# A transformer layer on one core: 31 warm-up products of 32 columns in place of nine of 128, a load in two halves, and a row block of x1 by column halves

## What is computed

```python
h = rmsnorm(x, norm1_g)
z = h @ w_in                       # queries, keys, values, mLSTM inputs and gates
mixed = concat(attention(z), mlstm(z))
x = x + mixed @ w_out              # called x1 below
h2 = rmsnorm(x, norm2_g)
logits = h2 @ w_router + b_router
top_v, top_e = top_k(logits, 4)
gates = softmax(top_v)
for e in range(32):                # the tokens that chose e
    gu = h2[tokens] @ w_gate_up[e] + b_gate_up[e]
    gate, up = min(gu[:, :1024], 7), clip(gu[:, 1024:], -7, 7)
    act = gate * sigmoid(1.702 * gate) * (up + 1)
    y[tokens] += gates[tokens, e] * (act @ w_down[e] + b_down[e])
x = x + y
```

## Time and profile before

| | us |
|---|---|
| median of 3 runs | 1055.46 (1054.89 to 1055.58) |
| the profiled execution, its own time | 1055.73 |
| its span in the profile | 1053.9 |
| TensorE busy | 1037.1 |
| VectorE busy | 197.8 |
| ScalarE busy | 143.0 |
| DMA, mean over the span | 403 GB/s |

### The profile page before, as it was taken

How to read it: one execution, slowest core, us unless ns; L and a number is a source line. 1 busy time by engine, 2 the same in 40 slices (tenths; PEclk the granted TensorE clock), 3 DMA queues, 4 the chain that set the end, 5 groups by cost and what they waited for, 6 DMA issues and landing times.

```text
span 1053.9 us, 11929 instructions
## 1 busy us (share of the span) xinstructions
PE 1037.1 (98%) x4775; PEld 386.1 (37%) x4775; DVE 197.8 (19%) x500; ACT 143.0 (14%) x299; POOL 5.5 (1%) x23
## 2 busy tenths in 40 slices
PE   9999999999999999999999999999999999999997
PEld 5655543333333333333333333333333332333332
DVE  2162332111111111111111111111111111011111
ACT  2144431001111100100111111111110110001101
POOL 1000000000000000000000000000000000000000
PEclk9999999999999999999999999999999999999999
DMA  9964699999999999999999999999999999999997
GB/s 339 364 232 160 254 374 396 428 428 428 428 429 428 429 430 428 428 428 428 428 429 428 430 428 428 428 428 430 428 429 428 428 428 428 429 429 429 425 423 294
DMA packets 42026, 424.62 MB, mean 403 GB/s; under 512 B 6512, under 2 KB 7576, under 8 KB 16536
## 3 DMA queue, kind: packets, MB, share of 16 engines
q1 hardware_dynamic: 41848, 424.10, 96.1%
q10 hardware_dynamic: 160, 0.27, 0.1%
HBM read 423.31 MB, written 1.05 MB: 403 GB/s over the span
## 4 chain that ended last, share of the span: by engine, by line
PE 76%; SPq 16%; DMA 7%; issue 1%; ACT 0%; DVE 0%; POOL 0%; ACTq 0%; POOLq 0%
PE bank L1565 31%; PE bank L1601 16%; SPq L391 9%; PE bank L1175 7%; SPq L398 6%; DMA ring<-in_w_gate_up 5%; PE bank L1524 4%; PE bank L1484 4%; PE bank L1369 3%; PE bank L1422 2%; DMA ring<-in_w_down 2%; PE bank L1495 2%; PE bank L1585 1%; PE bank L1211 1%; PE bank L1576 1%
## 5 line engine op out<-in xcount | busy, mean ns | idle before, releaser
L1565 PE MATMUL bank<-ring,xe_t 128*64 128x512 f32 x2048 | 449.4, 594 | 8.2 <-DMA ring<-in_w_gate_up 7.6
L1565 PEld LDWEIGHTS bank<-ring,xe_t 128*64 128x64 f32 x2048 | 143.0, 137 | 311.0 <-issue 289.6
L1601 PE MATMUL bank<-ring,late 128*64 128x512 f32 x992 | 219.9, 595 | 0.1
L1601 PEld LDWEIGHTS bank<-ring,late 128*64 128x64 f32 x992 | 68.5, 137 | 127.3 <-issue 122.2
L1095 DVE TENSOR_SCALAR gate_c<-bank 128x512 f32<-128x512 f32 x32 | 22.1, 691 | 436.7 <-PE bank L1565 436.7
L775 ACT ACTIVATE s_sb<-bank 128x256 f32<-128x256 f32 x32 | 12.3, 383 | 459.5 <-PE bank L1576 459.5
L1175 PE MATMUL bank<-ring 128*128 128x512 f32 x160 | 72.0, 595 | 0.2 <-issue 0.2
L1524 PE MATMUL bank<-late,s_sb 64*128 64x512 f32 x256 | 63.6, 615 | 0.7 <-ACT late L791 0.7
L1484 PE MATMUL bank<-xres,pick 128*64 128x512 f32 x248 | 60.1, 605 | 0.0
L791 ACT ACTIVATE late<-bank 128x512 f32<-128x512 f32 x32 | 19.1, 597 | 228.2 <-PE bank L1601 228.2
L1093 DVE COPY row_of<-fold 128x64 f32 x31 | 6.0, 195 | 197.1 <-PE bank L1422 197.1
(11 more groups left out here) (210 smaller groups left out, 424.2 us busy)
## 6 DMA issues: line engine op xcount, KB each, us to landing
ring<-in_w_gate_up SPq DMA_DIRECT2D x124, 2048.0 KB, 35.9
ring<-in_w_down SPq DMA_DIRECT2D x59, 2048.0 KB, 32.9
ring<-in_w_in SPq DMA_DIRECT2D x5, 2048.0 KB, 14.7
ring<-in_w_gate_up SPq DMA_DIRECT2D x8, 1024.0 KB, 25.1
ring<-in_w_down SPq DMA_DIRECT2D x7, 1024.0 KB, 24.2
ring<-in_w_out SPq DMA_DIRECT2D x2, 2048.0 KB, 10.6
ring<-in_w_down SPq DMA_DIRECT2D x6, 512.0 KB, 24.0
ring<-in_attn_bias SPq DMA_DIRECT2D x1, 1536.0 KB, 17.8
```

Of the source, the lines that this page charges most:

```text
L1565: mm = pe.matmul(bank[h][c * CAP:(c + 1) * CAP, :], xe_t[:, k, :], w[:, k % RUN, at:at + BANK], start=False, stop=(k == KD - 1), skip_grou ...
L1601: mm = pe.matmul(dst[c * CAP:(c + 1) * CAP, :], turned[:, at:at + CAP], w[:, k % DRUN, c * BANK:(c + 1) * BANK], start=(k == 0), stop=(k = ...
```

## The change

Four edits. Nine warm-up products with 128 moving columns become 31 with 32, the stationary side being the same 128x128 `ones`. The first load of expert 2 (1 MB) is issued as two of 512 KB, each when its columns have been read. The last quarter of x1 (row block 1, column half 1) is added, turned and copied in two halves of 256 columns, the first copy by ScalarE and the second by VectorE, into banks 7 and 0. And around it some places move: `part_copy(1)` stands ahead of `rms_x(1)`, `sum_x(1)` stands inside the top-four code of row block 0, and of the two `dense` products (384 and 256 columns) one with 128 is left.

```diff
-WARM = (5, 4)
+WARM = (16, 15)
...
-                    sp.wait_ge(gu_row_used, 2 * round_no + h + 1)
-                    sp.dma_start(gu_half(s)[:, 0:1, :], rows[:, 0:1, :]).then_inc(ld_piece[s], 16)
+                    if h == 0:
+                        for q in range(2):
+                            sp.wait_ge(gu_row_used, 3 * round_no + q + 1)
+                            sp.dma_start(gu_half(s)[:, 0:1, q * FF:(q + 1) * FF],
+                                         rows[:, 0:1, q * FF:(q + 1) * FF]).then_inc(ld_piece[s], 16)
+                    else:
+                        sp.wait_ge(gu_row_used, 3 * round_no + 3)
+                        sp.dma_start(gu_half(s)[:, 0:1, :], rows[:, 0:1, :]).then_inc(ld_piece[s], 16)
...
             square_x(1, 0)
             part_copy(0)
+            act.wait_ge(h2_turned, 4)
+            act.activation(ht[:, 4:6, P:SEQ], bank[7][:, 0:SEQ].rearrange("p (k n) -> p k n", k=2), ACT.Copy).then_inc(turned_act, 1)
             square_x(1, 1)
-            act.wait_ge(h2_turned, 4)
-            act.activation(ht[:, 4:8, P:SEQ], bank[7][:, :].rearrange("p (k n) -> p k n", k=4), ACT.Copy).then_inc(turned_act, 1)
+            part_copy(1)
             rms_x(1)
-            part_copy(1)
...
+            def add_last_x():
+                dve.wait_ge(mixed, 2 * T)
+                for i in range(2):
+                    xs = xres[:, T - 1, BANK + i * SEQ:BANK + (i + 1) * SEQ]
+                    dve.tensor_tensor(xs, bank[ACC[2 * T - 1]][:, i * SEQ:(i + 1) * SEQ], xs, ALU.add).then_inc(x1_ready, 1)
...
-            add_x(1, 1)
-            sum_x(1)
+            add_last_x()
+            dve.wait_ge(h2_turned, 5)
+            dve.tensor_copy(ht[:, 6:8, P:SEQ], bank[0][:, 0:SEQ].rearrange("p (k n) -> p k n", k=2)).then_inc(turned_dve, 1)
...
                 dve.max(top_v[:, t, :], lg[:, t, :]).then_inc(top_max, 1)
+                if t == 0:
+                    sum_x(1)
...
-                    pe.matmul(bank[1][:, 0:P], ones[:, :], ident[:, :], start=True, stop=True)
+                    pe.matmul(bank[1][:, 0:NE], ones[:, :], ident[:, 0:NE], start=True, stop=True)
...
-            turn_x(1, 1)
+            for i in range(2):
+                pe.wait_ge(x1_ready, 2 * T + i)
+                for k in range(2):
+                    c = 4 + 2 * i + k
+                    mm = pe.transpose(bank[(7, 0)[i]][:, k * P:(k + 1) * P], xres[:, T - 1, c * P:(c + 1) * P], ident[:, :])
+                mm.then_inc(h2_turned, 1)
             fold_parts(0)
-            dense(3 * P)
             logit_part(1, 1)
-            dense(SEQ)
+            dense(P)
             fold_parts(1)
...
+                        if n == 0 and k == 0 and h == 0:
+                            mm.then_inc(gu_row_used, 1)
```

More of the change, by code:

```diff
@@ L100, in loads_before @@
     return TURN_OF[n, k] // PIECES
-IN_HALVES = (piece_of(2, 0), piece_of(2, 1), piece_of(2, GUN))
-PIECE_LOADS = [len(range(s, KINDS * NE, PIECES)) + (s in IN_HALVES) for s in range(PIECES)]
+MORE_LOADS = {piece_of(2, 0): 2, piece_of(2, 1): 1, piece_of(2, GUN): 1}
+PIECE_LOADS = [len(range(s, KINDS * NE, PIECES)) + MORE_LOADS.get(s, 0) for s in range(PIECES)]
 END_PARTS = {(NE - 2, 0): (0, 2), (NE - 2, 1): (0, 2, 3), (NE - 1, 0): (0, 1, 3), (NE - 1, 1): (0, 2, 3)}
@@ L719, in square_x @@
             def square_x(t, c):
-                act.wait_ge(x1_ready, 2 * t + c + 1)
+                act.wait_ge(x1_ready, 2 * t + c + 1 + t * c)
                 if t + c:
@@ L1404, in logit_part @@
                     k = 4 * half + g
+                    if t and k == 6:
+                        pe.wait_ge(turned_dve, 2)
                     mm = pe.matmul(bank[ACC[t]][g * NE:(g + 1) * NE, 0:P], wr[:, k, :], ht[:, k, t * P:(t + 1) * P],
@@ L1502, in start_sum @@
                     pe.wait_ge(bank6_read, 1)
-                    pe.wait_ge(x1_ready, 4)
+                    pe.wait_ge(x1_ready, 2 * T + 1)
                     pe.wait_ge(top_max, T)
@@ L1557, in gate_up @@
                     if k % RUN == 0:
-                        halves = int(n >= 2 and s in IN_HALVES)
-                        pe.wait_ge(ld_piece[s], 16 * (PIECE_LOADS[s] * round_no + LOADS_A_LAP * lap + loads_before(n, k // RUN) + halves) + 16)
+                        more = MORE_LOADS.get(s, 0) if n >= 2 else 0
+                        pe.wait_ge(ld_piece[s], 16 * (PIECE_LOADS[s] * round_no + LOADS_A_LAP * lap + loads_before(n, k // RUN) + more) + 16)
                     if n >= NE - 2 and k == KD - 1:
@@ L1594, in down @@
                     if k % DRUN == 0:
-                        halves = int(n >= 2 and s in IN_HALVES)
-                        pe.wait_ge(ld_piece[s], 16 * (PIECE_LOADS[s] * round_no + LOADS_A_LAP * lap + loads_before(n, GUN + k // DRUN) + halves) + 16)
+                        more = MORE_LOADS.get(s, 0) if n >= 2 else 0
+                        pe.wait_ge(ld_piece[s], 16 * (PIECE_LOADS[s] * round_no + LOADS_A_LAP * lap + loads_before(n, GUN + k // DRUN) + more) + 16)
                     elif (n, k // DRUN, k % DRUN) in ld_end:
```

2 lines of the change are left out of this document (1 added, 1 removed).

## The result

| | before | changed |
|---|---|---|
| median, us | 1055.4 (5 runs, 1054.89 to 1055.58) | 1066.22 (5 runs, 1065.96 to 1067.44) |
| ratio | | 1.0107, 95% interval 1.0095 to 1.0118 |
| the profiled execution, its span | 1053.9 | 1065.6 |

The changed kernel is 1.1% slower. That is outside the predicted range; of the cases in the prediction it is the first rival, the clock that does not rise.

What follows compares the result with a forecast made beforehand. The end was taken as set by when the load stream becomes continuous, which TensorE's first 150 us delay, and by losses at the very end. +5.1 (warm-up) - 1.0 (halves, router included) = +4.1, median 1059.6 us; range 1057.1 to 1065.8.

Steps and rivals of the forecast that it cites:

- the first rival: Warm-up: TensorE's clock does not rise under narrow products; +9.2 to +11.2, less 1.0, giving 1063.7 to 1065.7 us; chance 0.2.
- now the sum, with the level rising at 8.1 as before: Warm-up: 14 products at 0.43 us until 8.1, 17 at 0.22 after; transposes at 12.1, TensorE's program shifted +5.1 us.
- the other 17 products: Warm-up products after the clock's rise at 8.1 us, claimed to take 17 x 0.22 = 3.7 us.
- their 0.5 back: Transposes of x: run at the full clock level, some 0.6 us instead of 1.1, giving 0.5 us back.
- weight loads fill the rest: Warm-up: argument against the clock not rising, that weight loads occupy TensorE where narrow products stream fewer columns.
- no stretch of the router at the full level fell: Router: argument against the clock not rising, that stretches with many narrow products kept the full level.
- the price of a narrow product: Warm-up: a 32-column product costs two weight loads, 0.43 us at the lower clock level, 0.22 at the full one.
- instruction blocks: Instruction fetch: 22 more products add 88 instructions and move the blocks; cost taken as nothing.
- The rival of cheap products: Warm-up: a product costs by its columns, 0.11 us, all hidden; -1.0, to 1054.5, at most 1053.6 us; chance 0.2.
- The first load in halves: Expert 2's first load: earlier issue recovers lost stream; -1.0 us, between +0.3 and -1.9, router's delay included.
- the overhead of 3.6 us: Expert 2's first load: a 2 MB load landed after 8.5 us, 4.9 of it at 428 GB/s, leaving 3.6 overhead.
- The router: Router with x1's last quarter in halves: expert 0 starts 0.3 us later, between 0 and 0.4.

Runs made afterwards that it cites:

- part 4: Kernel before with eleven 128-column warm-up products, `ones` on both sides, starting at about 1.2 us, instead of nine: 1054.97 us, ratio 0.9997.

## Why the prediction was wrong

**The step that failed** is "now the sum, with the level rising at 8.1 as before". I had taken the moment of rise from a start-up with 128 moving columns and used it for one with 32. The 31 wide products do exactly what the sum says (+5.25 in the start of expert 0 for +5.1); the 31 narrow ones leave TensorE at the lower level to 21.5 us. By this the other 17 products cost 0.44 instead of 0.22 (+3.7), the transposes don't get their 0.5 back, and 4.5 projection pairs run at 0.85 instead of 0.43 (+1.93): 6 us more than forecast. The first rival had this priced at +9.2 to +11.2 before the halves, and 10.99 were measured. What was wrong was its chance. The argument against it, "weight loads fill the rest", is what the runs contradict: at one number, pace and weight load the level was up before 6.5 us with 32 moving columns and at 12.9 with 8. And "no stretch of the router at the full level fell" was evidence on how long the upper level is kept, not on what brings it.

**Right:** the price of a narrow product (0.44 measured, 0.43 forecast, whatever its 32, 64 or 128 columns); that TensorE's first 150 us have no slack, so that each microsecond goes through to the end; instruction blocks at nothing, though the page of the profile now has 13 transfers instead of 12. The rival of cheap products is refuted by the warm-up rows.

**The first load in halves**, forecast -1.0, gave nothing: between 0 and +0.3 in the medians with the wide warm-up (the -1.0 had the router's delay in it). The step in it that failed is the overhead of 3.6 us between issue and landing, which I had taken as a time during which nothing flows. The packets begin 1.0 after the issue, while other engines still work off the load before. The end of the range at which nothing is gained, +0.3, is where it came out. The forecast also had the first load of expert 2 issued 1.4 behind the start of expert 0; its own numbers give 1.1 (158.0 less 156.87, since the router's 0.3 moves both), and 1.12 were measured (168.52 less 167.40).

**The router**, forecast +0.3, gave -0.16 in the changed kernel and -0.2 alone (156.37 against 156.57, of which 0.05 is the start). I had set VectorE's instructions end to end; in the trace a dependent or small one starts up to 0.1 before its predecessor's end, and the second chain no longer waits 0.36 for its logits, which was the larger part.

## What to carry to other kernels

A warm-up has two jobs, to fill time and to raise TensorE's clock, and the two can come apart. In these runs a float32 product with a 128-column stationary side filled the same time with 32, 64 or 128 moving columns, but with nine of them the level rose at 12.7, 11.5 and 8.1 us. Whoever narrows or cuts such products must look at the first wide instructions behind them, and read the level from spacings where the clock column says nothing. When a forecast takes over a moment (a level, a landing) from the old trace, ask what brought it there, and whether the change removes that. The time from issue to landing of a transfer is no idle time: look at when its first packet starts.

## What was not expected of the hardware

When TensorE's clock rose to the upper level, in the profile of each run, and what TensorE did before:

| warm-up | stationary columns | moving columns | us a product | transposes start | level up at |
|---|---|---|---|---|---|
| before, 9 | 128 | 128 | 0.43 | 6.5 | 8.1 |
| 9 | 128 | 64 | 0.43 | 6.4 | 11.5 |
| 9 | 128 | 32 | 0.43 | 6.3 | 12.7 |
| 31, changed kernel | 128 | 32 | 0.43 | 15.6 | 21.5 |
| 31 | 128 | 32 | 0.43 | 15.6 | 21.9 |
| 31 | 128 | 128 | 0.43, then 0.22 | 12.3 | 8.1 |
| 11, from 1.2 us on | 128 | 128 | 0.43 | 6.5 | before 6.5 |
| 31 | 32 | 32 | 0.107 | 6.5 | before 6.5 |
| 31, changed kernel | 32 | 32 | 0.107 | 6.4 | 9.8 |
| 36 | 32 | 32 | 0.107, then 0.063 | 6.6 | 5.2 |
| 36, changed kernel | 32 | 32 | 0.107 | 6.5 | 8.3 |
| 31 | 32 | 8 | 0.107 | 6.4 | 12.9 |

A product's time is read here between the starts of two that follow each other.

The moment of the rise isn't the same in two programs with one warm-up: with the nine wide products the eight transposes took 1.30, 1.30, 1.39, 1.62 and 1.80 us in the chains of five profiles, so that the level came up between 7.4 and 8.4, and the small products of 32 moving columns have 5.2 to 9.8 in seven. By the Trainium skill (TensorE: Matmul & The Clock Gate, section What's actually happening) this point varies from run to run; the traces agree, with these numbers. Among the five it is worth 0.1 us (the first projection starts between 8.50 and 8.60); a level that is up before the transposes brings 0.5 (8.07, part 4), one that comes at 9.8 costs 0.7 in the first eight pairs (4.34 in place of 3.67).

At the lower level a pair of weight load and matmul with 32 stationary columns takes 0.053 us with 32 and with 8 moving columns, where 128 stationary columns make it 0.21. The Trainium skill (the same page, section LDWEIGHTS) makes a load's time go with its columns; by it, 32 columns would take 27 ns, an estimate. The traces agree in the proportion, 0.053 being a quarter of 0.21, but at this level both are twice what the Trainium skill gives; at the upper level its figure fits, with 0.11 for 128 columns. Whether the 0.053 is the weight load or a least time of a pair, no run here shows.
